# Work of the next stage carried over two borders of a fused block kernel

## The reference

```python
hx = rms_norm(x, norm_pre1) * (1 + sc1x) + sh1x          # and hc for the context
rw, z, xbc, dt, gate = split(h @ w_in)                   # one wide input projection
# a recurrence with a matrix state per head (32 heads of 64), both directions
ya = rwkv7_branch(centred_token_shift(rw, mu), states of the context, ...)
# a state-space branch: 8 groups of 4 heads, both directions
xbc = silu(conv5(xbc) + conv_b)
dt  = softplus(dt + dt_bias); log_a = -exp(a_log) * dt
yb  = gated_group_rmsnorm(ssd(x * dt, log_a, B, C) + d_skip * x, z)
# mixing of the two branches by two gates
m   = sigmoid(g_a) * (ya @ w_a) + sigmoid(g_b) * (yb @ w_b)
x   = x + g1 * rms_norm(m @ w_o)
# experts: 8 heads, the best 16 of 128*128 experts each, rows gathered
x   = x + g2 * rms_norm(sum gate * gelu(h2 . u[expert]) * v[expert])
```

## Time and profile before

| what | value |
|---|---|
| time of three runs | 4279.43, 4294.98, 4297.5 us, median 4294.98 |
| profiled execution: its time | 4289.09 us |
| profiled execution: its span | 4287.4 us |
| PE busy in it | 3803.7 us (89%) |
| DVE, ACT, POOL busy in it | 2030.7, 731.1, 786.6 us |
| stages, by their first instructions | recurrence's last two turns 1486 to 1583.5, branch to 2261.4, mixing to 2842, gathers to the end |

### The profile page before, as it was taken

How to read it: one execution, slowest core, us unless ns; L and a number is a source line. 1 busy time by engine, 2 the same in 40 slices (tenths; PEclk the granted TensorE clock), 3 DMA queues, 4 the chain that set the end, 5 groups by cost and what they waited for, 6 DMA issues and landing times. The chain is left out here.

```text
span 4287.4 us, 81251 instructions
## 1 busy us (share of the span) xinstructions
PE 3803.7 (89%) x35655; PEld 2320.0 (54%) x35655; DVE 2030.7 (47%) x3409; ACT 731.1 (17%) x1318; POOL 786.6 (18%) x755
## 2 busy tenths in 40 slices
PE   7999999999999969999998999988777777777777
PEld 3466666666666645666667888566223322222223
DVE  1355555555555636767770000034554554554541
ACT  2223222322232202222220000011111111111101
POOL 3000000000000000000010000004444444444541
PEclk9999999999999979999999999999999999999999
DMA  9211111111111026655635444537999999999996
GB/s 378 83 36 47 46 48 36 48 46 48 36 48 46 26 60 200 199 178 181 197 113 185 149 157 177 186 131 284 404 398 424 406 405 424 404 405 424 405 423 249
DMA packets 408825, 872.93 MB, mean 204 GB/s; under 512 B 16557, under 2 KB 250687, under 8 KB 341311
## 3 DMA queue, kind: packets, MB, share of 16 engines
q0 software_dynamic: 73728, 536.90, 30.3%
q1 hardware_dynamic: 243072, 284.82, 20.3%
q10 hardware_dynamic: 91710, 46.43, 4.0%
HBM read 863.87 MB, written 4.23 MB: 202 GB/s over the span
## 5 line engine op out<-in xcount | busy, mean ns | idle before, releaser
L2421 PE MATMUL ps<-w_tail,diag 128*128 128x512 f32 x2048 | 969.8, 621 | 310.1 <-DMA w_tail<-in_peer_v,ixv 272.3
L2421 PEld LDWEIGHTS ps<-w_tail,diag 128*128 128x128 f32 x2048 | 385.0, 196 | 894.7 <-issue 553.0
L955 PE MATMUL ps<-hT,w_pair 128*128 128x512 f32 (+1 forms) x1536 | 634.1, 540 | 3.6 <-PEq L217 2.2
L1661 PE MATMUL ps<-hT,w_group 128*128 128x256 f32 (+1 forms) x1536 | 512.0, 487 | 0.0
L2273 DVE SCALAR_TENSOR_TENSOR junk<-w_tail,hT 128x2048 f32<-128x2048 f32 x128 | 293.5, 2293 | 299.5 <-DMA w_tail<-in_peer_u,ixu 298.8
L2273 DVE SCALAR_TENSOR_TENSOR junk<-ybT,hT 128x2048 f32<-128x2048 f32 x128 | 293.5, 2293 | 268.2 <-DMA ybT<-in_peer_u,ixu 266.4
L2176 POOL DMA_INDIRECT w_tail<-in_peer_v,ixv x256 | 298.0, 1164 | 550.9 <-PE ps L2421 488.2
L1661 PEld LDWEIGHTS ps<-hT,w_group 128*128 128x128 f32 x1536 | 287.2, 190 | 174.2 <-issue 153.6
L955 PEld LDWEIGHTS ps<-hT,w_pair 128*128 128x128 f32 x1536 | 268.5, 190 | 179.9 <-issue 156.3
L2340 ACT ACTIVATE diag<-ident,coef 128x128 f32<-128x128 f32 x256 | 101.5, 402 | 1004.7 <-PE ps L2421 994.5
L671 POOL TENSOR_TENSOR bonus<-Kh 128x256 f32<-128x256 f32 x16 | 11.7, 734 | 1184.4 <-DVE Kh L892 1184.4
(11 more groups left out here) (378 smaller groups left out, 4623.6 us busy)
## 6 DMA issues: line engine op xcount, KB each, us to landing
w_mod_piece<-in_w_mod SPq DMA_DIRECT2D x128, 512.0 KB, 4.9
w_pair<-in_w_in SPq DMA_DIRECT2D x48, 1024.0 KB, 6.1
w_group<-in_w_in ACTq DMA_DIRECT2D x44, 1024.0 KB, 7.4
w_mod_ring<-in_w_mod SPq DMA_DIRECT2D x16, 2048.0 KB, 12.6
w_tail<-in_w_in SPq DMA_DIRECT2D x7, 4096.0 KB, 14.5
w_tail<-in_w_branch_a SPq DMA_DIRECT2D x4, 4096.0 KB, 14.5
w_tail<-in_w_branch_b SPq DMA_DIRECT2D x4, 4096.0 KB, 14.5
w_tail<-in_w_out SPq DMA_DIRECT2D x4, 4096.0 KB, 13.8
```

The source lines that it names most:

```text
L955: last = mm(ps[:, 4, t0:TOK], w[:, m % 2, k, :], hT[:, k, t0:TOK], start=(k == 0), stop=(k == KC - 1))
L1661: last = mm(out, w[:, m % SLOTS_W, k, :], hT[:, k, t0:TOK], start=(k == 0), stop=(k == KC - 1))
L2421: last = nc.tensor.matmul(ps[:, 4 * n + c, :], diag[:, k % 2, :], vb[k % NB][:, c * 512:(c + 1) * 512], start=False, stop=False)
```

## The change

- All weight slots are one tile, `w_slots` (64 KB in each partition), which lives through all stages: the recurrence's two slots and several of its other buffers (KR, RK, WU, F, Mt, Ct), the branch's four slots and its w_mod pieces, padded buffer and row buffer, and the mixing's two slots lie in it. w_dt lies in the recurrence's buffer eng.
- **Border 1.** At the end of turn 14 the sync queue loads tile x0 of group 0, w_dt, and tile x1. In turn 15 the pieces that did nothing do x0's 16 steps (`next_tile`, bank 4), in turn 16 the 16 steps of the step sizes (`step_sizes`, bank 5). In the branch both are gone; the step sizes' transposes stand behind two steps of x1, and their sums behind all of x1.
- **Border 2.** The first product of the mixing, ga of block 0, is done in the branch's turn 8 by `first_gate`, in the places of the pieces. Its weights are loaded into the four slots as tiles B, C, z0 and z of group 7 are done, and the second gate's 4 MB after them into the other half. The mixing starts with gb; the vec transpose and all of the key transposes stand behind it, as do ACT's copy of vec and its way to DRAM.

```diff
+                    if a_ == PAIRS - 1:
+                        sp.wait_ge(*PA.by("r", a_))
+                        sp.dma_start(w[0], w_in[:, :, X0:X0 + P]).then_inc(ss_loads[0], 16)
+                        sp.wait_ge(*VA.by("Ah1", a_))
+                        sp.dma_start(w_dt, w_in[:, :, DT0:GA0]).then_inc(dt_w, 16)
+                        sp.wait_ge(*PA.by("v", a_))
+                        sp.dma_start(w[1], w_in[:, :, X0 + P:X0 + 2 * P]).then_inc(ss_loads[1], 16)
...
+                def next_tile(k0, k1):
+                    if k0 == 0:
+                        pe.wait_ge(ss_loads[0], 16)
+                        pe.wait_ge(*AA.by("keep1", PAIRS - 1))
+                    for k in range(k0, k1):
+                        last = mm(ps[:, 4, :], w[0][:, k, :], hT[:, k, :], start=(k == 0), stop=(k == KC - 1))
+                    if k1 == KC:
+                        last.then_inc(*ss_pe.did("x0"))
...
+                TILE_AT = {("k", 8): (0, 2), ("k", 10): (2, 4), ("k", 12): (4, 5), ("k", 13): (5, 6), ("k", 15): (6, 7),
+                           ("r", 0): (7, 9), ("r", 9): (9, 11), ("r", 12): (11, 13), ("v", 0): (13, KC)}
+                STEPS_AT = {("k", 0): (0, 1), ("k", 2): (1, 2), ("k", 4): (2, 3), ("k", 5): (3, 4), ("k", 6): (4, 5), ("k", 7): (5, 6),
+                            ("k", 8): (6, 7), ("k", 10): (7, 8), ("k", 12): (8, 9), ("k", 13): (9, 10), ("k", 15): (10, 11),
+                            ("r", 12): (11, 13), ("v", 0): (13, KC)}
...
                     def piece(name, k0, k1):
                         if A:
                             project(name, p, k0, k1)
+                        elif B and (name, k0) in TILE_AT:
+                            next_tile(*TILE_AT[name, k0])
+                        elif not B and (name, k0) in STEPS_AT:
+                            step_sizes(*STEPS_AT[name, k0])
...
+                for c in range(4):
+                    sp.wait_ge(*PA.by(TILES[2 + c], GROUPS - 1))
+                    sp.dma_start(w[c], w_in[:, :, GA0 + c * P:GA0 + (c + 1) * P]).then_inc(first_in[c], 16)
+                sp.wait_ge(*VA.by("c3_4", GROUPS - 1))
+                sp.wait_ge(*PB.by("mod", GROUPS - 1))
+                sp.dma_start(slots[:, 1, :].rearrange("p (k n) -> p k n", n=512), w_in[:, :, GA0 + D:GA0 + D + 512]).then_inc(mg_w[1], 16)
...
-                    bank = lambda n: (5 * i + n) % 2
+                    bank = lambda n: (5 * i + n) % 2 if (i, n) != (0, 0) else 4
...
-                pe.wait_ge(w_sem, 16)
-                for k in range(KC):
-                    last = mm(ps[0:2 * SH, 4, :], w_dt[:, k, :], hT[:, k, :], start=(k == 0), stop=(k == KC - 1))
-                last.then_inc(proj, 1)
+                def first_gate(m0, m1):
+                    for m in range(m0, m1):
+                        c, k = divmod(m, KC)
...
+                        last = mm(ps[:, c // 2, (c % 2) * SEQ:(c % 2 + 1) * SEQ], w[c][:, k, :], hT[:, k, SEQ:TOK], start=(k == 0), stop=(k == KC - 1))
+                    if m1 == 4 * KC:
+                        last.then_inc(*PG.did("ga"))
+
+                GATE_AT = {(1, 4): (0, 6), (1, 8): (6, 12), (1, 12): (12, 14), (2, 0): (14, 18), (2, 2): (18, 24), (3, 0): (24, 36), (3, 8): (36, 4 * KC)}
...
-                pe.wait_ge(vec_done, 4)
-                nc.tensor.transpose(ps[0:4 * KC, 4, 0:P], vec[:, :, :].rearrange("p v k -> p (v k)"), ident[:, :]).then_inc(vec_tr, 1)
                 loads = [0, 0]
                 for i in range(BL):
                     if i:
                         pe.wait_ge(w_in[0], 32 * i)
                         pe.wait_ge(*AG.by("ga", i - 1))
-                    product(0, hT[:, :, SEQ:TOK], 0, first=(i == 0)).then_inc(*PG.did("ga"))
+                        product(0, hT[:, :, SEQ:TOK], 0).then_inc(*PG.did("ga"))
+                    pe.wait_ge(w_in[1], 32 * i + 16)
+                    if i:
+                        pe.wait_ge(*AG.by("gb", i - 1))
+                    product(1, hT[:, :, SEQ:TOK], 2).then_inc(*PG.did("gb"))
                     if i == 0:
+                        pe.wait_ge(vec_done, 4)
+                        nc.tensor.transpose(ps[0:4 * KC, 4, 0:P], vec[:, :, :].rearrange("p v k -> p (v k)"), ident[:, :]).then_inc(vec_tr, 1)
```

158 lines of the change are left out of this document (90 added, 68 removed).

## The result

| what | before | after |
|---|---|---|
| median of the runs timed side by side | 4296.24 us (4279.43 to 4299.41) | 4233.23 us (4227.53 to 4236.89) |
| ratio of the times, 95% interval | | 0.986 [0.9839, 0.988] |
| profiled execution: its time, its span | 4289.09, 4287.4 us | 4234.48, 4232.7 us |
| PE busy in it | 3803.7 us (89%) | 3804.2 us (90%) |
| gather packets of 8 KB, mean time each | 315.96 ns | 313.72 ns |

63 us are gone, with the same work on PE: idle time went. The forecast was 50.5. The range held it, but two of its terms were off in opposite directions, and most of what follows is about these two.

A forecast was written before the change was run, and what follows sets the result against it. The gathers were taken as DMA-bound, with PE holes at two borders: 28.1 + 22.4 = 50.5 us off the profiled 4289.1 gives 4238.6, or 4244 with the 5.9 us to the median; range 4222 to 4268.

The forecast's parts named there:

- Rival A: Recurrence, turns 15 and 16: the clock stays full through both, in all 58.4 us saved, 4236 us; chance 20%.
- Border 2, 22.4 us: Branch's last turn into the mixing: first gate product fills PE's waits, so product A starts 22.4 us earlier.
- x1 to B, 19.4 us: Branch's start: x1, its cold start, transposes, sums and a 1.6 us wait for ACT before B, together 19.4 us.
- Turn 15, +4.4 us: Recurrence: carried steps overrun the gaps by 4.6 us; with the clock's effect at r9 the turn grows 4.4.
- Turn 16, +1.9 us: Recurrence's last turn: rounds +1.1, outputs -1.1, steps at r12 +1.2, mean and variance products -1.0, steps at v0 +1.7.
- rival C: Recurrence, turns 15 and 16: the clock stays at half through both, recurrence grows 27 us, 4265 us; chance 12%.
- Border 1 in all, 28.1 us: Recurrence into branch: B can begin 34.4 us earlier, less 6.3 by which the recurrence grows, a gain of 28.1 us.
- From A on everything follows PE and then the gathers, so it moves as one: From the mixing's product A to the end: the stretch is unchanged, so the whole gain carries through.
- case E: Mixing and gathers: the shared weight arena's new places slow the gathers, at 5% giving 4317 us; chance 3%.
- the border about 6 us later: Border after the recurrence: expected about 6 us later in the new trace, as the recurrence grows by 6.3.
- The thin covers: Step-size chain, DVE's 3 us of slack in group 0, or x0's load fails: up to 10 us, 4254; chance 10%.
- The rule on the clock: Trainium skill: idle gaps between matmuls throttle PE's clock; by that alone steps closing gaps would hold full clock through both turns.

The follow-up runs named there:

- x_arena: Against the kernel before: only the shared tile for all weight slots, no work carried over a border; 4272.81 us, ratio 0.9953.
- x_sums: Against the changed kernel: sums of the step sizes placed ahead of the last four steps of x1; 4234.08 us in a single execution.
- x_places: Against the kernel before: 128 bytes left free ahead of w_pair, iota_f allocated behind the expert stage's big buffer; 4273.5 us, ratio 0.9946.
- x_best: Against the changed kernel: carried steps moved to gaps, five x1 steps at turn 16's end, sums two steps before x1's end; 4225.02 us, ratio 0.9832.
- x_align256: Against the changed kernel: 128 unused bytes ahead of the shared weight tile; 4252.29 us, ratio 0.9895.
- x_pad_behind: Against the changed kernel: 128 bytes left free behind the shared weight tile, slots unmoved, later buffers moved; 4225.75 us, ratio 0.9833.

## Why the prediction was right, and where it was not

**It was right in time (4244 against 4233.2, inside 4222 to 4268), and its centre was 11 us high.** Some of that nearness is luck. The borders alone gave some 45 us, about 4250; another 20 came from a term that the sum had at nothing. The range would have held either time. Rival A's 4236 is nearer still, and its mechanism, a clock that stays full through both turns, did not happen. Step by step:

- *Border 2, 22.4 us.* The last turn and the mixing went from 421.8 to 398.7 us: 23.1, and within 0.1 us the same in eight executions. The single steps held as well: turn 8 is 44.3 us long (some 44 expected) at clock 1.00, the path through DVE hidden, product A 30.4 us behind the border (30.6). It held because its terms are counts of records at a known pace or gaps to be filled. (2.5 of the 23.1 us stand in x_arena too.)
- *x1 to B, 19.4 us.* 19.65 measured, and the wait for ACT that was expected at 1.6 us is 1.52; x_sums showed that it is what it was taken for, by removing it.
- *Turn 15, +4.4 us.* (The overruns listed make 4.5, not 4.6.) In the two profiled executions it grew by 5.8. Over six executions with the order of before and six with that of the change, start of turn 15 to the end of the readouts is 61.1 to 64.2, mean 62.75, against 65.7 to 67.6, mean 66.7: +4.0. The sum held. The clock story behind it held in the profiled execution (the steps at r9 at double price, the solve 2.0 us shorter where 1.1 was said), and didn't in the second. A fall in the turn's first 12 us (one or two windows of 4 us below full, the lowest at 0.55 to 0.78) came in ten of the fourteen executions, of both orders; in the profiled one of the change it cost 1.3 us (the transposes of KR stand 9.6 us into the turn, 8.3 before).
- *Turn 16, +1.9 us. This is the step that failed.* From the readouts to the first product of the branch it is 43.5 to 43.7 us in the six of before, of which 7.6 lie behind the border, so 36.0; and 39.7 to 41.8 in the six of the change, mean 41.3. It grew by 5.3. By the rows of the profiled execution: the rounds grew by 2.0 (+1.1 expected), since a round with a step takes 1.38 us at full clock and not 1.28; the 2 us charged for a start at half clock were right (the first two such rounds take 2.52 and 2.18, 1.9 over). The outputs take 6.0 us (1571.1 to 1577.1) where 5.9 less 1.1 was expected. Half clock for the second half of them had been reckoned with; what had not is the issue wait of 1.14 us, which the outputs of turn 16 show in all eight executions with carried steps there (0.3 to 1.2 us) and in none of the six without. The two steps behind them take 3.67 us and not 1.8, so that from there to the border it grew by 3.8 and not 1.9: the forecast had the clock back by then, and it was still at half. So the largest part was rival C, half clock, in one place, and the next an instruction wait that no case had.
- *Border 1 in all, 28.1 us.* By the third column, 186.7 in the mean of six executions against 162.5 in that of five with the change's start of the branch: 24.2, so 3.9 us are missing. Turn 16 is 3.4 of them.
- *"From A on everything follows PE and then the gathers, so it moves as one", and the recurrence ahead of turn 15 untouched: wrong, by some 20 us.* The shared tile's new places stood in the sum at nothing, and case E had seen that it touches the bound but gave it one direction only, slower, at 3%. x_arena priced it at 20 us faster, and x_places got the same from places alone, without the change. It had two parts of about equal size: the gathers' packets, 2.2 ns each (about 9 us), and PE's issue waits in the recurrence (28 to 20 us). The prediction had named "gathers of another pace" as a sign of being wrong, and it showed: 315.96 to 313.72 ns.
- *The sign to look for, "the border about 6 us later":* it was, 1589.7 against 1583.5. It agreed for the wrong reason: turn 15 had begun 5.5 us earlier (in the second execution 11.9, against 4.9 later in the second of before), and the two turns had grown by 11.6.
- *The thin covers* (case D): PE never waited for x0's weights, and the branch between its marks is 564.6 us in both, so DVE's 3 us of slack were enough.

Sum of the parts: 24 us from border 1, 20.6 from border 2 beyond x_arena, and x_arena's own 20 are 65, where 63 (by the ratio 60, 52 to 69) were measured; so nothing is known to be left over.

**The rule on the clock.** It was weighed in the prediction, and rival A with it. In the changed kernel PE was busy 93.7 of 109.6 us of turns 15 and 16, and its clock still fell at least twice in every one of the six executions with its order (behind the readouts and in the outputs); but it held in turn 15 of the changed kernel's second execution, whose rows above have a window with PE busy 2.90 of 4 us at full clock. So neither "no gaps, no fall" nor "small products, a fall" is what these runs show. (The prediction's "without gaps" was too strong as well: in its rows 2 PE is idle for 0.6 to 0.7 of each 4 us.) x_best held it longest, with 512-column steps between the small products at every level.

## What to carry to other kernels

Filling PE's waits at a stage's border with the next stage's first products pays what it promises if the weights can be on their way early and if each carried product is costed at the clock of its place: where the granted clock was low before, take double price until a trace shows otherwise. When a change re-lays buffers, cost that too, with both signs; run it alone (the new layout with the old order of work) before crediting its gain to anything else, and try a kernel that is bound by loads with its big buffers moved by 64 or 128 bytes. Read a stage in several executions before giving a few us of it to a cause.

## What was unexpected of the hardware

- **The place of a buffer in the core's memory changes the pace of loads into it.** 128 unused bytes ahead of the weight slots move the ratio to before from 0.9858 to 0.9895; 8 KB gather packets take 313.7 or 317.7 ns, 1 MB weight loads land in 5.8 or 6.2 us, 4 MB in 13.8 or 14.4. By single packets it is sharper: 98% of the gather packets into w_slots take exactly 309 ns in the changed kernel, and 33 to 38% in x_align256, and the 512-byte packets of the recurrence's weights take 28.5 to 28.7 ns in ten traces and 30.5 to 30.7 in the other four. Adding up the tile sizes in order of allocation, and taking the memory's start to be a multiple of 256, the slots lie at 128 over a multiple of 256 bytes in the fast kernels, at a multiple in x_align256, and w_pair of before at a multiple too. Of the gathers' two buffers in before, w_tail lies at 192 over and ybT at 128. These are few places, and x_pad_behind puts ybT on a multiple with no loss, so a rule doesn't follow. The Trainium skill ("DMA: Bandwidth & Descriptors", "How a descriptor splits into AXI transactions") has it that a transaction has to start on a multiple of 256 bytes, so that a descriptor which doesn't start there fetches from the boundary below it. It speaks of reads, and these buffers are written. Were it taken over to the place written, x_align256 would be the fastest of the changed kernel's layouts, and it is the slowest. The measurement decides: here an aligned slot was not the better one.
- **PE's issue waits go with it, and they are waits for instructions**: 27 to 31 us of the recurrence in the four executions with slow weight loads, 19 to 22 in the ten with fast ones. All 198 that are longer than 0.8 us end 1.2 to 1.7 us behind a packet of the DMA queue "q8 instruction". How the place of the weight slots slows these packets is not shown.
- **The clock's fall is not fixed by the program.** Two executions of the changed kernel differ in whether it falls behind turn 15's small products at all; the turn is 1.6 us shorter in the one where it doesn't. Two of before differ too: ahead of the solve the clock is full in one up to 37 us into the turn, and below full in six of the first eight windows of 4 us in the other. And x_align256, where it held behind the small products, has the longest turn 15 of the six (67.65 us), as its clock was low for two windows at the start.
